# Two rests of a weight split move behind the gated products in the stick-breaking layer's VectorE order

## The reference, cut to what matters

```python
def branch_b(h, w_in, w_out):
    z = h @ w_in
    q, k, v, gate = jnp.split(z, [B_WIDTH, 2 * B_WIDTH, 3 * B_WIDTH], axis=-1)
    o = stick_breaking_attention(q, k, v).astype(h.dtype)
    return (o * jax.nn.silu(gate)) @ w_out
```

## Time and profile before

| | |
|---|---|
| median of 3 runs | 903.99 us (903.72 to 904.41) |
| profiled execution, its own time | 904.42 us |
| its span, first to last instruction | 902.7 us |
| TensorE busy (weight load) | 893.0 us (861.6) |
| VectorE busy | 551.5 us |
| ScalarE busy | 430.4 us |
| GpSimd busy | 56.4 us |
| DMA | 153.06 MB, mean 170 GB/s |
| mean granted clock of TensorE | 0.998 of full speed |

### The profile page before, as it was taken

One profiled execution on the slowest core, in us unless ns is written; L12 is line 12 of the kernel. 1 busy time (PEld: TensorE's weight loads), 2 busy tenths in 40 slices (PEclk: granted clock), 3 DMA queues, 4 the chain that ended last, 5 costly groups with the idle time before them and its releaser, 6 DMA issues.

```text
span 902.7 us, 17891 instructions
## 1 busy us (share of the span) xinstructions
PE 893.0 (99%) x7182; PEld 861.6 (95%) x7182; DVE 551.5 (61%) x752; ACT 430.4 (48%) x685; POOL 56.4 (6%) x85
## 2 busy tenths in 40 slices
PE   9999999999999999999999999999999999999997
PEld 9999999999999999899999999999999999988886
DVE  6577667666755767785646464555646355545546
ACT  6556455645555344385454443535444444435421
POOL 1322112312200000000000000000000000000000
PEclk9999999999999999999999999999999999999999
DMA  9676465546442555425353434444453534454622
GB/s 351 232 236 180 154 209 134 156 160 190 131 155 114 187 187 191 183 69 211 142 187 139 180 145 169 156 147 178 139 186 139 186 144 165 156 218 156 233 93 94
DMA packets 25256, 153.06 MB, mean 170 GB/s; under 512 B 3410, under 2 KB 3938, under 8 KB 8708
## 3 DMA queue, kind: packets, MB, share of 16 engines
q1 hardware_dynamic: 21600, 142.19, 43.1%
q0 software_dynamic: 2896, 7.70, 4.5%
q10 hardware_dynamic: 724, 2.66, 0.8%
HBM read 150.36 MB, written 2.18 MB: 169 GB/s over the span
## 4 chain that ended last, share of the span: by engine, by line
PE 96%; DMA 1%; DVE 1%; SPq 1%; ACT 0%; issue 0%; DVEq 0%
PE bank L336 72%; PE bank L716 10%; PE bank L495 2%; PE bank L453 2%; DMA work<-chunks 1%; PE bank L661 1%; PE bank L660 1%; PE bank L663 1%; PE bank L628 1%; PE bank L587 1%; PE bank L601 1%; PE bank L470 1%; PE bank L629 0%; PE bank L588 0%; PE bank L471 0%; PE bank L702 0%
## 5 line engine op out<-in xcount | busy, mean ns | idle before, releaser
L336 PE MATMUL bank<-x_hi,w_hi 128*128 128x272 f32 (+1 forms) x1472 | 425.1, 289 | 0.0
L336 PE MATMUL bank<-x_hi,w_lo 128*128 128x272 f32 (+1 forms) x1472 | 421.5, 286 | 0.0
L336 PE MATMUL bank<-x_lo,w_hi 128*128 128x272 f32 (+1 forms) x1472 | 421.4, 286 | 0.0
L1078 DVE TENSOR_TENSOR w_lo<-raw,w_hi 128x2048 fp32r<-128x2048 f32 x126 | 291.0, 2313 | 209.8 <-ACT w_hi L795 177.3
L795 ACT ACTIVATE w_hi<-raw 128x2048 fp32r<-128x2048 f32 x114 | 218.0, 1913 | 156.9 <-PE bank L336 104.5
L336 PEld LDWEIGHTS bank<-x_hi,w_hi 128*128 128x128 f32 x1472 | 277.4, 188 | 0.9 <-issue 0.2
L336 PEld LDWEIGHTS bank<-x_hi,w_lo 128*128 128x128 f32 x1472 | 277.4, 188 | 0.0
L336 PEld LDWEIGHTS bank<-x_lo,w_hi 128*128 128x128 f32 x1472 | 277.1, 188 | 0.0
L336 PE MATMUL bank<-og_hi,w_hi 128*128 128x272 f32 x240 | 70.1, 292 | 0.0
L336 PE MATMUL bank<-og_hi,w_lo 128*128 128x272 f32 x240 | 69.4, 289 | 0.0
L336 PE MATMUL bank<-og_lo,w_hi 128*128 128x272 f32 x240 | 69.1, 288 | 0.0
(11 more groups left out here) (247 smaller groups left out, 1008.4 us busy)
## 6 DMA issues: line engine op xcount, KB each, us to landing
raw<-chunks SPq DMA_DIRECT2D x128, 1024.0 KB, 4.8
work<-bias_table POOLq DMA_DIRECT2D x8, 512.0 KB, 5.7
work<-chunks SPq DMA_DIRECT2D x4, 512.0 KB, 12.6
work<-bias_table POOLq DMA_DIRECT2D x8, 256.0 KB, 6.9
work<-ln_rows ACTq DMA_DIRECT2D x1, 2048.0 KB, 6.9
out<-work SPq DMA_DIRECT2D x8, 256.0 KB, 2.4
h<-xT SPq DMA_DIRECT2D x2, 544.0 KB, 9.2
raw<-chunks SPq DMA_DIRECT2D x4, 256.0 KB, 4.9
```

Of the source, the lines that this page charges most:

```text
L336: last = mm(o, l, r, start=(kt == 0 and n == 0), stop=(kt == KT - 1 and n == 2))
L1078: V.tensor_tensor(lo_part, raw[:, half, :, :], hi_part.bitcast(f32), ALU.subtract) \
```

## The change

It takes the rests of the two halves of P + 5 (the next pass's key chunk) out of their places before and behind the gates, and puts both behind the gated products and their rests. Nothing else is edited; the instructions and waits of TensorE, ScalarE, GpSimd and SyncE are the same.

```diff
                 split_lo(P + 4, 1, True)
-                split_lo(P + 5, 0, True)
                 for u in range(2):
                     dve.wait_ge(gateb_exp, 2 * i + u + 1)
...
                      .then_inc(tile_free[u], 1)
-                split_lo(P + 5, 1, True)
                 for u in range(2):
                     dve.wait_ge(pv_done, PV_A + 2 * i + u + 1)
...
                                     ALU.subtract).then_inc(og_lo_ready, 1)
+                split_lo(P + 5, 0, True)
+                split_lo(P + 5, 1, True)
```

## The result

| | before | after |
|---|---|---|
| median | 903.86 us (903.72 to 904.41, 4 runs) | 938.55 us (931.37 to 941.43, 4 runs) |
| ratio | | 1.037, 95% interval 1.0349 to 1.0391 |
| profiled execution, span | 904.42 us, 902.7 us | 941.43 us, 939.7 us |
| granted clock, mean | 0.998 | 0.976 |

A forecast was written before the change was run, and what follows sets the result against it. The prediction took TensorE's uninterrupted matmuls to bound the kernel. Gated products gained 0; seven stalls of 2.94 us made 20.6 us on 904.42, which stands 0.43 above the median, giving 924.6 us (+2.3%), range 919 to 935.

The forecast's parts named there:

- What bounds the kernel: Stick-breaking passes: uninterrupted TensorE matmuls, 52.22 us a pass; the key chunk's wait for the query copy has 2.25 us margin.
- Gates and gated products: VectorE in each pass: gates no earlier, gated products 2.20 us earlier, gain on the path 0.
- The load and the stall: Query-to-key hand-over: late 4.73 us load delays ScalarE's rounding and the copy behind it; TensorE stalls 2.9 us each time.
- What is late next, and how many: Later loads and output stage: lateness used up within the pass, one stall each, seven hand-overs, 0 in the output stage.
- The sum: Whole kernel: 7 x 2.94 = 20.6 us added to 904.42, less 0.43, giving 924.6 us, +2.3%.
- rival (a): TensorE's clock falls in the seven stalls, 0 to 3 us more each; 935 us at 1.5, 945 at all; 14%.
- signs of being wrong: TensorE waiting for w_lo or twice a pass, pass clock below 0.98, or no DMA wait before ScalarE's first rounding.
- (c): Value chunk's first half in its slot by 600.5, so the copy is in time: not slower, 904 us; 3%.
- (d): ScalarE or VectorE reach the pair earlier than traced, leaving 1 to 2 us per pass: 911 to 918 us; 3%.
- (b): Lateness not used up: key tile 0's copy holds the value chunk too, 1 to 3 us per pass, 931 to 945; 5%.

The follow-up runs named there:

- e1: The changed kernel with ScalarE's two query-tile copies put ahead of its rounding of the value chunk's first half: 906.94 us, ratio 1.0034 to the kernel before.
- e4: Against the kernel before, both rests behind the gates but ahead of the gated products (only the first moves): 903.99 us, ratio 1.0001.
- e2: The changed kernel plus 22 unneeded matmuls between query and key chunk in each loop pass, filling the hole: 925.10 us, ratio 1.0234 to the kernel before.
- e3: Against the kernel before, only the second rest moved behind the gated products, the first left ahead of the gates: 904.04 us, ratio 1.0004.
- e6: The changed kernel plus 8 unneeded matmuls between query and key chunk, 0.9 us of the hole filled: 928.80 us, ratio 1.0275 to the kernel before.

## Why the prediction was right and wrong

**What bounds the kernel**, and that TensorE's wait for the query copy is the place: right, as the waits, e1 and e4 show.

**Gates and gated products**: right. The last og_lo is followed by the pair at 495.07, and the earlier products gave nothing.

**The load and the stall**: right within 0.2 us. Counted from the start of the first rest, the prediction had the rounding 7.19 us later (596.15 to 603.34) and TensorE 9.51 us later; measured are 7.37 and 9.70. The load took 4.90 us from issue to rounding and not 4.73. The sum of the section, 20.6 us, stands against the 21.1 us of e2, where the clock is held. The 6.15 us for 1 MB in the section "Bandwidth" of the Trainium skill's "DMA: Bandwidth & Descriptors", measured on transfers issued from GpSimd, would by an estimate have put the rounding 1.4 us later than the 4.73 did. The 4.90 us of this load, issued from SyncE, sides against it again.

**What is late next, and how many**: right in the main. Seven stalls, one a pass, and the output stage without a loss: its first rounding is at 852.83, 15.50 us behind its start, as before (815.83 less 800.32 is 15.51). That the lateness is used up inside the pass is best seen in e2, where the clock is held: the gate chunk's rounding waits for its load until 675.38, 6.75 us behind the start of the key chunk (the prediction had 6.84, 612.5 less 605.66), and the first key copy, at 677.99, waits for TensorE alone.

**The step that failed** is the clock. The sum put it at nothing. It stood only in rival (a), which had its mechanism and place written down, but got 14%, with 3.0 us a stall as the most it could cost and 1.5 us taken. Measured, the clock fell behind all seven stalls and cost 1.5 to 2.7 us each, 2.3 on average: 16.4 us in the profiled execution, 13.5 us by the medians (938.55 less 925.10). The total by the rival's own rule of 0 to 3 us holds the measured 938.55; its middle value of 935 was low, and the range ended there. The prediction's own signs of being wrong show it: the granted clock in the passes (434 to 837) is 0.95, where it had drawn the line at 0.98, and the period is 56.9 to 58.1 us and not 55.1.

Was there evidence in the rows of before? They have holes of 1.1 us with the clock kept, and none between 1.1 and 2.8 us. But the fall at the end of the kernel was set aside as lying behind the last matmul, without asking how long behind. The last matmuls of before, and those of e3 with the window around them:

```profile
896.61 1.95 PE L761 MATMUL bank<-h 2*128 2x512 f32 x4 [0.45 <-ACT h L1061]
...
896.25 2.39 PE L761 MATMUL bank<-h 2*128 2x512 f32 x4 [0.45 <-ACT h L1061]
897.00:898.00 1.00, 1.00 (x3) 0.18 (x1) 1.00 (x2) 0.56 (x1) 0.00 (x0) 0.82 0.00 0
```

In before they end at 898.56, and the clock is down at 899.5: TensorE had stood still for 0.9 us, behind waits of 1.11 and 0.45 us with a single matmul between them. In e3, behind the same two waits, the clock falls at about 897.6, while the last four matmuls are still under way. So the trace of before already showed a fall without 2.8 us of standing still in one piece, and the weight should not have gone to "kept".

The page "TensorE: Matmul & The Clock Gate" of the Trainium skill, in "Why this matters for your kernels", asks for no idle gaps beyond a length that it names between bursts of matmuls. The trace agrees that such gaps bring the lower clock, but not on their length: every hole here, 2.97 us at the most, is shorter than the one the page warns of, and still the clock fell seven times in seven behind 2.33 to 2.97 us and three times in seven behind the 1.42 to 1.91 us of e6. The measurement decides.

Rivals (c) and (d) did not come about. Of (b), only e1 shows something.

Still open: why the lower clock lasted 3.4 us behind the first two stalls and 6.8 us in and behind the other five. The rows show only that in the five it had fallen before TensorE resumed, and in the first two only after; the three falls of e6 came after it too, and lasted 3.4 us. No run changed this alone. Open, too, is why of two holes of the same length in e6 one was followed by a fall and the other not.

## What to carry to other kernels

When work is pushed later on an engine that seems to have time, follow what its end releases (here a buffer, a 1 MB load, a rounding), and then look at what is queued behind the last of these on its engine: the loss came from a copy that had nothing to do with the moved work. If the chain ends in an idle TensorE, price the idle time and the clock apart, and take a hole of about 2 us or more in a kernel that keeps TensorE full as one that may lower the clock: here, behind holes of 2.3 to 3.0 us, that cost nearly as much again as the waiting. If the hole can't be closed, try filling it with matmuls that nothing needs: here that was 13.5 us cheaper than the hole (e2).

## What had not been expected of the hardware

The clock may fall behind a hole of 1.9 us, in some hand-overs and not in others of the same length in one execution (1.89 and 1.91 us). It may fall up to 1.5 us after TensorE is at work again (559.93 to about 561.4 in e6, 504.77 to about 506.1 in the changed kernel). It may fall without any hole of that length, while matmuls run, behind waits of 1.11 and 0.45 us (e3, at about 897.6). And such a kernel loses its steadiness: 931 to 941 us where it had repeated within 0.7 us.
